# Five norms of a two-part network: products that start on weighted h, with the root multiplied in behind them

## The reference, cut to what matters

```python
def rmsnorm(x, g):
    return x * rsqrt(mean(x * x, axis=-1) + 1e-6) * g

h = x
h = h + even_mixer(rmsnorm(h, ev_norm_mix), ...)
h = h + cross_attn(rmsnorm(h, xa_norm[0]), mem, ...)      # keys, values: rmsnorm(mem, xa_norm_mem) @ wkv
h = h + swiglu(rmsnorm(h, ev_norm_ffn), ...)              # (silu(x @ gate) * (x @ up)) @ down
h = h + conformer_conv(rmsnorm(h, od_norm_mix), ...)      # x @ pw1, gate, 31-tap conv, norm, @ pw2
h = h + cross_attn(rmsnorm(h, xa_norm[1]), mem, ...)
h = h + moe_swiglu(rmsnorm(h, od_norm_moe), ...)          # 8 experts, 2 for each token
...
result = rms_norm(x, final_g)                             # the end of the second block
```

## Time and profile before

| | us |
|---|---|
| median of 3 runs (lowest, highest) | 2438.81 (2438.15, 2439.09) |
| the profiled execution, whole | 2440.72 |
| its span, first to last instruction | 2438.9 |
| TensorE busy | 2341.8 (96%) |
| VectorE busy | 687.9 (28%) |
| ScalarE busy | 376.7 (15%) |
| mean granted clock of TensorE | 0.978 of 2.4 GHz |
| read from memory | 641.7 MB, 264 GB/s over the span |

### The profile page before, as it was taken

The page is one execution under the profiler, slowest core; times in us unless marked ns, Lnnn a source line. Parts: engine busy times, 40 slices in busy tenths (PEclk is TensorE's granted clock), DMA queues, the critical chain, the costliest instruction groups (busy, mean ns, idle before and its releaser), DMA issues.

```text
span 2438.9 us, 34641 instructions
## 1 busy us (share of the span) xinstructions
PE 2341.8 (96%) x14916; PEld 1345.8 (55%) x14916; DVE 687.9 (28%) x1507; ACT 376.7 (15%) x813; POOL 1.2 (0%) x9
## 2 busy tenths in 40 slices
PE   8899999999999999999998999998989999989997
PEld 6777888888577333333333333335766336746433
DVE  2565121139765101011010101011232122273122
ACT  2101100010111111110110111111132111163211
POOL 0000000000000000000000000000000000000000
PEclk9899999999999999999999999998999999999998
DMA  9489245374366798999999999996622995832690
GB/s 319 164 296 359 72 166 214 132 265 141 115 223 250 295 380 339 374 385 408 405 409 405 408 405 409 395 395 254 235 69 75 338 317 157 214 114 75 213 357 36
DMA packets 281384, 645.13 MB, mean 265 GB/s; under 512 B 14699, under 2 KB 99969, under 8 KB 281217
## 3 DMA queue, kind: packets, MB, share of 16 engines
q1 hardware_dynamic: 278444, 637.64, 71.2%
q10 hardware_dynamic: 2773, 5.11, 0.6%
HBM read 641.66 MB, written 1.05 MB: 264 GB/s over the span
## 4 chain that ended last, share of the span: by engine, by line
PE 88%; DVE 6%; SPq 2%; ACT 2%; issue 1%; DMA 1%; ACTq 0%; DVEq 0%
PE bank L1613 20%; PE bank L1299 20%; PE bank L1715 11%; PE bank L1650 7%; PE bank L1538 6%; PE bank L1550 3%; PE bank L1319 3%; DVE att L3372 2%; PE bank L1642 2%; SPq L1205 2%; PE bank L1775 2%; PE bank L1734 1%; PE bank L1701 1%; PE bank L1861 1%; PE bank L1348 1%
## 5 line engine op out<-in xcount | busy, mean ns | idle before, releaser
L1613 PE MATMUL bank<-ring,xn 128*32 128x512 f32 (+1 forms) x3520 | 465.9, 594 | 2.3 <-DMA ring<-od_moe_gu 2.3
L1299 PE MATMUL bank<-xn,ring 128*128 128x256 f32 x2048 | 452.0, 383 | 3.3 <-ACT xn L2286 1.1
L1299 PEld LDWEIGHTS bank<-xn,ring 128*128 128x128 f32 x2048 | 392.0, 192 | 60.3 <-issue 8.1
L1613 PEld LDWEIGHTS bank<-ring,xn 128*32 128x32 f32 (+1 forms) x3520 | 140.2, 115 | 304.2 <-issue 301.5
L1715 PE MATMUL bank<-ring,att 128*32 128x512 f32 x2208 | 247.9, 593 | 1.3 <-ACT att L2416 1.3
L2979 DVE TENSOR_TENSOR sq<-att,bank 32x512 f32<-32x512 f32 x70 | 48.0, 686 | 414.4 <-ACT att L2427 412.9
L1715 PEld LDWEIGHTS bank<-ring,att 128*32 128x32 f32 x2208 | 72.3, 110 | 160.1 <-issue 159.7
L1538 PE MATMUL bank<-xn,ring 128*128 128x256 f32 x704 | 152.8, 379 | 0.0
L1538 PEld LDWEIGHTS bank<-xn,ring 128*128 128x128 f32 x704 | 134.1, 191 | 17.9
L2427 ACT ACTIVATE att<-bank 64x512 f32<-64x512 f32 (+1 forms) x123 | 72.4, 589 | 376.1 <-PE bank L1613 291.6
L2416 ACT COPY att<-bank 128x384 f32<-128x384 f32 (+1 forms) x72 | 29.9, 450 | 520.3 <-PE bank L1701 400.1
(11 more groups left out here) (352 smaller groups left out, 1968.7 us busy)
## 6 DMA issues: line engine op xcount, KB each, us to landing
ring<-od_moe_gu SPq DMA_DIRECT2D x196, 1024.0 KB, 15.5
ring<-od_moe_down SPq DMA_DIRECT2D x49, 2048.0 KB, 17.3
ring<-ada_w SPq DMA_DIRECT2D x24, 2048.0 KB, 8.2
ring<-moe_w_gate SPq DMA_DIRECT2D x32, 1024.0 KB, 11.6
ring<-moe_w_up SPq DMA_DIRECT2D x32, 1024.0 KB, 9.7
ring<-moe_w_down SPq DMA_DIRECT2D x16, 2048.0 KB, 13.8
z<-od_moe_gu SPq DMA_DIRECT2D x28, 1024.0 KB, 13.8
ring<-ev_w_in SPq DMA_DIRECT2D x10, 2048.0 KB, 20.4
```

The lines of the kernel that those rows point to most:

```text
L1299: mm = nc.tensor.matmul(ps[:, c * T:(c + 1) * T], kblk(b)[:, k, u * T + c * P:u * T + (c + 1) * P], x[:, k, :], start=k == 0, stop=k == KD ...
L1613: mm = nc.tensor.matmul(PSB[r.fill.b][j * w:(j + 1) * w, :], xn[:, k, at:at + w], rows_[:, half, c * WBLK:(c + 1) * WBLK], start=k == 0, s ...
```

## The change

At five norms (feed-forward, convolution block, second cross attention, experts, final) VectorE writes `raw`, h times the norm's weight, pair by pair behind the sums into `h`. The first products take `raw`. At the first three of them, units 0 and 1 do; the mean of squares is made between the halves of unit 0 and the roots are spread behind it. VectorE copies the spread root to `rstd` and multiplies both banks by it in place (`even`); it writes `xn` with four wide products for unit 2 and on. Readers of the two banks wait for `evened`. At the experts' norm the router and the turned tokens take `raw`, and the root, now a column with a token on each partition, is multiplied in at the copies; its spread goes. At the end `raw` is turned, ScalarE and VectorE copy two banks each with the root as a scale, and each half of the rows is stored by a transfer of its own, on ScalarE's and SP's queue.

At the first cross attention memory's part comes first. `norm_memory(0)` moves ahead of the block before, into the upper half of `z`; the mean of squares stands between keys and values, the spread behind the second value unit, and `xn` is written between ada steps. The products with zeros go at all six. `raw_unit`'s argument `middle` is called between the halves; `pe_mean_squares(st, 0)` issues no zeros. Cut to its core:

```diff
@@ -580,26 +582,42 @@
-def root_of(st, freed):
+def root_of(st, freed, bank=None):
...
-    st.fill = fill_turn(freed)
+    st.fill = fill_turn(freed) if bank is None else fill(bank, freed)
...
 def sum_of(st):
...
-def norm(h_at, to_xn=True, shifted=False, freed=None):
+def norm(h_at, to_xn=True, shifted=False, freed=None, bank=None):
...
-    st.h = h_at
+    st.h, st.raw = h_at, None
...
-    root_of(st, freed)
+    root_of(st, freed, bank)
...
+    return st
+def raw_norm(h_at, raw):
+    even = count(evened, 2)
+    st = norm(h_at, freed=(evened, even + 2))
+    st.even, st.raw, st.raws = even, raw, count(raw_ready, 4)
+    return st
+def column_norm(h_at, raw, bank=None):
+    st = Stage()
+    st.h, st.sq, st.xn, st.scaled = h_at, count(sq_ready, 4), None, None
+    root_of(st, (var_ready, counted(var_ready) + 1), bank)
+    st.sum, st.added = count(sum_ready, 1), 0
+    st.raw, st.raws = raw, count(raw_ready, 4)
@@ -789,7 +807,7 @@
 def memory_kv(l, beside=None):
...
-    st.memn = count(memn_ready, KD)
+    st.memn, st.at = count(memn_ready, KD), z[:, 8:16, :] if l == 0 else memn
@@ -797,7 +815,7 @@
 def cross(l, h_at, kv, beside, beside_out=None):
...
-    st.norm = norm(h_at)
+    st.norm = norm(h_at, bank=6) if kv is None else raw_norm(h_at, z[:, 8:16, :])
@@ -1142,8 +1160,8 @@
-final2 = norm(moe2[1].h)
-out_fills = [fill_turn((out_ready, i + 1)) for i in range(4)]
+final2 = column_norm(moe2[1].h, xn, 6)
+out_fills = [fill_turn((rows_out[i % 2], i // 2 + 1)) for i in range(4)]
@@ -1267,6 +1285,9 @@
+    sp.wait_ge(rows_out[1], 2)
+    sp.dma_start(out[0][P:2 * P, :], x_tok[:, 1, :]).then_inc(out_landed, 16)
+    sp.wait_ge(out_landed, 32)
@@ -1305,6 +1328,26 @@
+    def raws(st):
+        return lambda k: pe.wait_ge(raw_ready, st.raws + k // 2 + 1)
+    def raw_unit(st, i, b, u, f):
+        if i == 0:
+            unit(b, u, f, st.raw, raws(st), lambda: pe_mean_squares(st, 0))
+            spread_root(st)
+        elif i == 1:
+            unit(b, u, f, st.raw)
+        else:
+            unit(b, u, f, xn, normed(st) if i == 2 else None)
+    def pe_raw_linear(st, of):
+        for i, (b, u, f) in enumerate(st.units):
+            if u == 0:
+                landed(b)
+            raw_unit(of, i, b, u, f)
+            sums_beside(st, i)
@@ -1364,10 +1410,13 @@
+    def spread_root(st):
+        pe.wait_ge(root_ready, st.root + 1)
+        spread_roots(PSB[st.fill.b][:, T:2 * T], 0)
     def pe_roots(st):
...
-        pe.wait_ge(root_ready, st.root + 1)
-        spread_roots(PSB[st.fill.b][:, T:2 * T], 0)
+        spread_root(st)
@@ -1504,40 +1553,52 @@
-    def pe_memory_kv(st):
+    def pe_memory_kv(st, of=None):
         def ready(k):
...
-        pe_linear(st.k, memn, ready)
-        pe_token_linear(st.v, memn)
+        pe_linear(st.k, st.at, ready)
+        if of is None:
+            pe_token_linear(st.v, st.at)
+        else:
+            pe_mean_squares(of, 0)
+            pe_token_linear(st.v, st.at, lambda: spread_root(of))
     def pe_cross(st, own_kv):
-        pe_norm(st.norm)
...
-            pe_memory_kv(st.kv)
+            pe_memory_kv(st.kv, st.norm)
         def q_unit(i):
...
-            unit(b, u, f, xn, normed(st.norm) if i == 0 else None)
+            if own_kv:
+                unit(b, u, f, xn, normed(st.norm) if i == 0 else None)
+            else:
+                raw_unit(st.norm, i, b, u, f)
...
-    def gate_up(x, w=T, src=xn, ready=None):
+    def gate_up(x, of=None):
...
+            src = xn if of is None or j >= 2 else of.raw
+            ready = None if of is None else {0: raws(of), 2: normed(of)}.get(j)
...
+                if half and j == 0 and of is not None:
+                    pe_mean_squares(of, 0)
...
-                    if ready is not None and j == 0 and half == 0:
+                    if ready is not None and half == 0:
...
-                    mm = nc.tensor.matmul(ps[:, half * T:half * T + w], kblk(b)[:, k, j * P:(j + 1) * P],
-                                          src[:, k, 0:w], start=k == 0, stop=k == KD - 1)
+                    mm = nc.tensor.matmul(ps[:, half * T:(half + 1) * T], kblk(b)[:, k, j * P:(j + 1) * P],
+                                          src[:, k, :], start=k == 0, stop=k == KD - 1)
...
+            if j == 0 and of is not None:
+                spread_root(of)
@@ -2033,27 +2094,25 @@
-    pe_norm(norm_ffn)
...
-        gate_up(x, ready=normed(norm_ffn) if s == 0 else None)
+        gate_up(x, norm_ffn if s == 0 else None)
...
-    pe_norm(norm_od)
-    pe_linear(pw1, xn, normed(norm_od))
+    pe_raw_linear(pw1, norm_od)
...
-    pe_norm(norm_moe)
...
-    pe_route(route1, router1, E1, normed(norm_moe))
-    tokens_by_row(xtok_fills, route1, E1)
+    pe_route(route1, router1, E1, raws(norm_moe), x=norm_moe.raw)
+    pe_mean_squares(norm_moe, 0)
+    tokens_by_row(xtok_fills, route1, E1, norm_moe.raw)
@@ -2253,14 +2312,14 @@
-    pe_norm(final2)
-    normed(final2)(KD - 1)
...
-            mm = nc.tensor.transpose(ps[:, k * P:(k + 1) * P], xn[:, i % 2 * 4 + k, i // 2 * P:(i // 2 + 1) * P],
+            raws(final2)(i // 2 * 4 + k)
+            mm = nc.tensor.transpose(ps[:, k * P:(k + 1) * P], final2.raw[:, i // 2 * 4 + k, i % 2 * P:(i % 2 + 1) * P],
...
+    pe_mean_squares(final2, 0)
@@ -2393,14 +2454,18 @@
     def act_cross(st, own_kv):
...
+        if own_kv:
+            copy_units(st.kv.k, pairs(kT))
...
-            act_memory_kv(st.kv)
-        act_attention(st.att, lambda i: copy_unit(st.q, pairs(z), i))
-    def act_gates(units, first=0, last=None, w=T):
+            copy_units(st.kv.v, tokens())
+        act_attention(st.att, lambda i: copy_unit(st.q, pairs(z), i, None, None if own_kv else st.norm))
+    def act_gates(units, first=0, last=None, w=T, of=None):
...
+            if of is not None and i < 2:
+                act.wait_ge(evened, of.even + i + 1)
@@ -2468,9 +2533,14 @@
-    def act_tokens_by_row(fills):
+    def act_tokens_by_row(fills, of=None):
...
-            nc.scalar.copy(xn_tok[:, i // 2, i % 2 * 512:(i % 2 + 1) * 512], full(f)).then_inc(xtok_ready, 1)
+            to = xn_tok[:, i // 2, i % 2 * 512:(i % 2 + 1) * 512]
+            if of is None:
+                nc.scalar.copy(to, full(f)).then_inc(xtok_ready, 1)
+            else:
+                act.wait_ge(root_ready, of.root + 1)
+                nc.scalar.activation(to, full(f), ACT.Copy, scale=roots[:, 1, i // 2:i // 2 + 1]).then_inc(xtok_ready, 1)
@@ -2586,6 +2656,8 @@
+        else:
+            act.wait_ge(evened, norm_od.even + 2)
@@ -2723,11 +2795,13 @@
-    for i, f in enumerate(out_fills):
-        nc.scalar.copy(x_tok[:, i // 2, i % 2 * 512:(i % 2 + 1) * 512], full(f)).then_inc(out_ready, 1)
-    act.wait_ge(out_ready, 4)
-    act.dma_start(out[0].rearrange("(c p) d -> p c d", p=P), x_tok).then_inc(out_landed, 16)
-    act.wait_ge(out_landed, 16)
+    act.wait_ge(root_ready, final2.root + 1)
+    for half in range(2):
+        nc.scalar.activation(x_tok[:, 0, half * 512:(half + 1) * 512], full(out_fills[2 * half]), ACT.Copy,
+                             scale=roots[:, 1, 0:1]).then_inc(rows_out[0], 1)
+    act.wait_ge(rows_out[0], 2)
+    act.dma_start(out[0][0:P, :], x_tok[:, 0, :]).then_inc(out_landed, 16)
+    act.wait_ge(out_landed, 32)
@@ -2789,14 +2863,45 @@
+    def raw_pair(st, g, i):
+        dve.wait_ge(h_ready, st.h - 3 + i)
+        for k in (2 * i, 2 * i + 1):
+            ins = nc.vector.tensor_scalar(st.raw[:, k, :], h[:, k, :], g(k), None, ALU.mult)
+        ins.then_inc(raw_ready, 1)
     def squares_behind(st, i):
-        if st is not None and i >= 2:
+        if st is None:
+            return
+        if st.raw is not None:
+            raw_pair(st, st.g, i)
+        if i >= 2:
...
-    def normalise(st, g, shifted=False, given=None):
+    def even(f):
+        ps = full(f).rearrange("p (c t) -> p c t", c=2)
+        nc.vector.tensor_tensor(ps, ps, twice(rstd), ALU.mult).then_inc(evened, 1)
+    def normalise_raw(st, first):
...
+        chain(nc.vector.tensor_copy(rstd, root))
+        even(first)
+        dve.wait_ge(raw_ready, st.raws + 4)
+        for u in range(4):
+            at = slice(2 * u, 2 * u + 2)
+            nc.vector.tensor_tensor(xn[:, at, :], st.raw[:, at, :], twice(root), ALU.mult).then_inc(xn_ready, 2)
+        dve.wait_ge(xn_ready, st.xn + KD)
+    def normalise(st, g, shifted=False, given=None, rooted=False):
+        if rooted:
+            dve.wait_ge(spread_ready, st.spread + 1)
+            root = PSB[st.fill.b][:, T:2 * T]
+        else:
+            add_squares(st)
+            root = root_rows(st)
@@ -2926,19 +3031,25 @@
     def norm_memory(l):
...
-            nc.vector.tensor_scalar(memn[:, k, :], memT[:, k, :], col("xa_norm_mem", l * KD + k), None,
+            nc.vector.tensor_scalar((kv1 if l else cross0.kv).at[:, k, :], memT[:, k, :], col("xa_norm_mem", l * KD + k), None,
...
     def dve_cross(st, own_kv, then):
-        normalise(st.norm, vec("xa_norm", st.l * KD))
...
```

(46 more changed lines are left out.)

37 lines of the change are left out of this document (23 added, 14 removed).

## The result

The changed kernel took 2406.82 us (2403.69 to 2407.74 in four runs) against 2438.95 beside it: a ratio of 0.9863, with a 95% interval from 0.9846 to 0.9880. Forecast were 2416.5 and a range down to 2410. The direction is right; the gain is 33.1 us of span where 22.3 were reckoned, and the time lies outside the range.

What follows compares the result with a forecast made beforehand. TensorE was taken as the bound (88% of the span), with zero products at six norms to win back. Site gains and losses summed to 22.3 us, giving 2416.5 us; range 2411 to 2421, with the faster rivals 2410 to 2424.5.

Steps and rivals of the forecast that it cites:

- What every site keeps: At each norm, mean of squares (0.97 us) and spread (0.52) stay: 1.5 us of each gap; no wait inside a unit.
- Feed-forward: At the feed-forward norm, the gap of 5.8 us less the 1.5 that stay: gain 4.3 us.
- convolution block: At the convolution block's norm, the gap of 6.9 us less 1.5: gain 5.4 us, all passed on.
- experts' norm: At the experts' norm, choice of experts 5.0 us earlier, but counting waits for the slot constants: gain 3.3 us.
- banks: Third attention unit, second part: the shifted bank turn makes pair scores open a bank whose copy has just begun: -0.6 us.
- expert stage: First expert stage, load queue full (share 1.03): loads move with TensorE, so the experts' norm's gain is not given back.
- The load queue: Rival, chance 0.10: in the first expert stage the queue gives the experts' norm's 3.3 us back as idle time: 2419.8.
- First cross attention: There memory's projection starts at once: gap 9.6 us less 1.5, less about 0.8 waiting for a late ada step: gain 7.3.
- Second cross attention: There the norm gives 5.1 us, an ada-sum wait takes 3.2 and a clock fall 2.5: -0.6 in all.
- The rule that the forecast quotes from the Trainium skill: TensorE's clock: "the default state is throttled, and activity releases the throttle"; it speaks against taking the zero products out.
- End: From the last sum into h to the final store: gain 3.2 us, the middle of two cases with the clock down.
- the row's 4.4: At the end, the store's time in the profile before, 4.4 us, kept because both halves are issued together.

Runs made afterwards that it cites:

- slots_early: The changed kernel with the slot constants fetched before the squares of the experts' norm instead of behind its root: 2403.42 us.
- memn_first: The kernel before plus 39 skipped zero products, with only memory's normed chunks moved ahead of the ada steps of the block before: 2424.59 us.
- cross0_old: The changed kernel with the first cross attention's norm as before, norm_memory(0) still moved ahead, and 111 skipped zero products: 2408.17 us.
- turns: The changed kernel with the first ada step beside the second cross attention done beside the first one instead: 2400.57 us.
- cross1_old: The changed kernel with the second cross attention's norm as before (root and xn first, with zero products) and 111 skipped zero products: 2405.91 us.
- no_zeros: The kernel before without the 17 zero products at each of five norms, with 124 zero products in a skipped block: 2443.54 us.
- pad_before: The kernel before with 39 zero products (78 instructions) in a block this input skips: 2431.05 us, 0.9967 of the kernel before.
- piece_before: The kernel before with 128 zero products (256 instructions, one whole piece of program) in the skipped block: 2441.08 us, 0.9994 of the kernel before.
- pad_after: The changed kernel with 88 zero products (176 instructions) in a block this input skips: 2415.43 us.
- piece: The changed kernel with 128 zero products (256 instructions, one whole piece of program) in the skipped block: 2407.27 us.

## Why the prediction was right and where it failed

*What every site keeps* was right: the small products move the shift by 0.8 to 0.9 and 0.4 to 0.5 us (0.97 and 0.52 were reckoned), the copy takes 0.42, the evening 0.70 and the wide `xn` 2.47; there is no wait inside a unit.

*Feed-forward, convolution block, experts' norm, banks, expert stage* came within 0.15 us each. The bound that released counting was named rightly (slot constants, 4.24 us of wait). The wait that the bank turn was to cost is there too, behind ScalarE's copy:

```profile
1760.07 0.60 PE L1487 MATMUL bank<-zeros 128*128 128x512 bf16 x2 [0.46 <-ACT vtok L2356]
```

The load queue kept nothing of the change: the shift is -23.31 at 831 and -23.24 at 1676 (this stage is 36% of the span, not half). So that rival falls here, but slots_early shows that there was little room left.

*First cross attention*: the 7.3 were there (the wait for the late step's sums was 0.47, not 0.8), and 1.7 more, because a stretch at 1.2 GHz behind the gap went with it. The step named the gap and not what follows a gap; it had priced just this at the second cross attention. It also read the gap as one thing. Its last 3.4 us had another cause, which memn_first and cross0_old show.

*Second cross attention*: mechanism right, wait 2.75 for 3.2, in all -1.1 for -0.6. The fall behind the new wait cost 3.4 us where 2.5 were taken. The other fall of 6.8 us, behind the wait on the softmax, stands in the kernel before too, at 728.6. turns bears this out, and cross1_old agrees. The rule that the forecast quotes from the Trainium skill (page "TensorE: Matmul & The Clock Gate", Part 1) agrees with the traces: at every gap of no_zeros the clock falls.

*End*: 4.7 for 3.2. The term that was mis-sized is the fall of the clock. I took the middle of the two cases with the clock down, 8.4 and 9.8 us from the last sum to the root. But the turned chunks ran in 3.12 us, and only the mean of squares, 1.87 for 0.97, paid for half clock. The root came 7.7 us after the last sum, between the 6.8 of full clock and the 8.4 of the milder case. The store went out in two halves, the later one 4.2 us before the end (2401.57 to 2405.8), so the row's 4.4 was a good price. From issue to landing the whole store took 4.0 us before; the halves, issued by ScalarE and SyncE, took 3.0 and 3.8, and the end waits for the later. The Trainium skill, page "DMA: Bandwidth & Descriptors", section "Anatomy of one DMA", gives its 2.0 us and 436 GB/s for transfers issued by GpSimd; the estimate of 3.2 us from them lies between the two halves, but under the one that counts.

*What failed the forecast* is a step that isn't in it. It took everything behind the last site as a rigid shift, with "a microsecond or two" for the clock. It put the places at which TensorE's program is fetched at nothing. But 177 instructions fewer move them: 1.7 us at the mean products, 4.9 at the small ones (a stall of 1.95, one of 0.49, and the half clock from 2128 to 2131, 0.52 in its window), of which 1.0 went again, because the fall of the clock at 2121.5 in the changed kernel lasts 10.2 us and its like in the kernel before, at 2152, 6.8. This is 5.6 of the 10.8 us that the forecast missed. The other parts are 1.8 at the first cross attention, 1.5 at the end, 2.1 of falls of the clock ahead of the first site, less 0.5 at the second cross attention; the rest is small change. By the medians the share is larger: of the gain of 32.1 us 23.8 are left with the stalls away on both sides, so 8.3 belong to them and to the half clock that follows. The two accounts don't agree in detail, since the falls elsewhere differ from one execution to the next. That 23.8 lies so near the 22.3 is in part luck: in the traces the six sites alone gave 25.9 where 22.9 were reckoned. The stalls were in the profile of before, 1.98 and 1.95 us of "issue" idle time amid equal products, in a place that the prediction doesn't read because the change doesn't touch it.

Left open: the 2.1 us ahead of the first site. Nothing that executes there on TensorE was changed; the half-clock stretches at 15 and 87 are shorter by 3.4 us each in the changed kernel, and of other lengths again in traces of other variants with the same work there. The sizes of these falls differ from one execution to the next, and cross0_old shows that they can hide more than 2 us of a site (3.8 lost there, 1.4 at the end). Nor was it tried why the jump ahead of the mean products costs 3.1 to 3.6 us in twelve of the fourteen traces, 2.1 in pad_before and 1.6 in piece_before, why a packet of the program comes late in some kernels, or why the kernel before spreads over 18 us; that the late pieces race with the loads of weights is only a guess. The Trainium skill, page "Advanced Engine Details and Errata", section "ISA Cache", gives lines of 16 KB for 256 instructions; the packets of q8 (16 KB, about 255 products and loads apart) agree.

## What to carry to other kernels

Fewer or more instructions on TensorE shift the pieces of its program everywhere behind the edit: look in the trace for idle time with cause "issue" amid equal short products, and before crediting or blaming an edit measure it again with padding in a block that is never executed. Price a gap of TensorE together with the half clock that follows it, and ask of each part of the gap what ended it: more than half of the largest gain here was one reordering on VectorE. Where first products no longer wait for a norm, see what VectorE has to do at that moment; moving two ada steps and one transfer won another 15.8 us.

## What the runs showed of the hardware

- TensorE's program comes in packets of 16 KB, one for about 247 executed instructions. A burst of short products (128 in 3.7 us) that crosses the end of a piece can stand still for 0.5 to 2.7 us; the eight stalls in the traces of before, pad_after and piece_before ended 1.3 to 1.6 us after a packet. Where the end falls decided over 8 to 10 us of the whole kernel (pad_before against piece_before, pad_after against piece).
- A stall of 2.7 us was followed by 14 us at 1.2 GHz, which cost 6.7 us (pad_after), a wait of 2.75 on a semaphore by 6.8 us, which cost 3.4 (the changed kernel): in both the fall of the clock cost more than the wait.
- Idle gaps of 5.8 to 9.6 us without zero products cost 2.5 us more each than with them, on average of five (no_zeros against pad_before).
